# Conditioning projections of a decoder step: from split fp32r products to plain fp32 matmuls in four column strips

## What is computed

```python
sh1, sc1, g1, sh2, sc2, g2 = split(silu(c) @ ada_w[layer] + ada_b[layer], 6)
h = rmsnorm(x, gain) * (1 + sc1) + sh1
x = x + g1 * mixer(h)
...
shift, scale = split(silu(c) @ kv_ada_w + kv_ada_b, 2)         # shared K/V
shf, scf = split(silu(c) @ final_ada_w + final_ada_b, 2)       # last norm
```

## Time and profile before

| | |
|---|---|
| median of 3 runs | 2059.22 us (2056.70 to 2061.25) |
| span of the profiled execution, first to last instruction | 2059.2 us |
| TensorE, VectorE, ScalarE busy | 91%, 75%, 61% of the span |
| GpSimd busy | 5% |
| HBM traffic over the span | 251 GB/s |
| expert loop, 1107 to 2032 us (first expert left out) | 925 us, clock 1.00, DMA 329 GB/s |

### The profile page before, as it was taken

How to read it: one execution, slowest core, us unless ns; L and a number is a source line. 1 busy time by engine, 2 the same in 40 slices (tenths; PEclk the granted TensorE clock), 3 DMA queues, 4 the chain that set the end, 5 groups by cost and what they waited for, 6 DMA issues and landing times.

```text
span 2059.2 us, 26798 instructions
## 1 busy us (share of the span) xinstructions
PE 1882.6 (91%) x9526; PEld 1462.0 (71%) x9526; DVE 1538.1 (75%) x2020; ACT 1251.1 (61%) x1490; POOL 101.5 (5%) x112
## 2 busy tenths in 40 slices
PE   5799996899898976976999999999999999999996
PEld 2696454888798734164787877878778787787784
DVE  5473777676585487263898989989899898898993
ACT  5553444566334434053777777777777777777773
POOL 2000010000000030001000000000000000000000
PEclk9897777999999859985999999999999999999998
DMA  9254693488444350433898998989989999899990
GB/s 312 82 195 157 233 316 131 149 277 270 164 153 155 123 206 1 162 129 119 287 363 319 340 363 303 359 320 341 366 304 355 336 329 364 300 359 335 328 355 21
DMA packets 230616, 518.84 MB, mean 252 GB/s; under 512 B 5187, under 2 KB 27817, under 8 KB 230546
## 3 DMA queue, kind: packets, MB, share of 16 engines
q1 hardware_dynamic: 226386, 504.42, 68.5%
q0 software_dynamic: 3856, 12.40, 1.7%
q10 hardware_dynamic: 304, 1.08, 0.2%
HBM read 509.91 MB, written 7.96 MB: 251 GB/s over the span
## 4 chain that ended last, share of the span: by engine, by line
PE 76%; DVE 10%; ACT 5%; issue 5%; DMA 3%; SPq 1%; DVEq 0%; POOL 0%; ACTq 0%; POOLq 0%
PE psum L609 18%; PE psum L611 18%; PE psum L610 18%; PE psum L581 3%; PE psum L582 3%; DVE w_lo L1374 2%; DMA ring<-in_moe_w_gate_up 2%; PE psum L954 2%; PE psum L852 2%; SPq L376 1%; PE psum L969 1%; PE psum L776 1%; DVE x L1462 1%; PE psum L599 1%; PE psum L705 1%
## 5 line engine op out<-in xcount | busy, mean ns | idle before, releaser
L1788 DVE TENSOR_TENSOR w_lo<-ring,w_hi 128x1024 fp32r<-128x1024 f32 x672 | 815.8, 1224 | 120.5 <-ACT w_hi L1326 109.4
L1326 ACT CAST w_hi<-ring 128x1024 fp32r<-128x1024 f32 x672 | 704.1, 1052 | 230.8 <-PE psum L611 230.8
L1374 DVE TENSOR_TENSOR w_lo<-ring,w_hi 128x1024 fp32r<-128x1024 f32 (+1 forms) x260 | 311.0, 1214 | 181.9 <-ACT w_hi L1068 181.0
L1068 ACT CAST w_hi<-ring 128x1024 fp32r<-128x1024 f32 (+1 forms) x260 | 265.7, 1040 | 249.8 <-PE psum L582 110.6
L609 PE MATMUL psum<-w_hi,xe_hi 128*128 128x512 f32 x896 | 371.1, 414 | 4.3 <-DVE w_lo L1788 4.3
L611 PE MATMUL psum<-w_hi,xe_lo 128*128 128x512 f32 x896 | 354.4, 396 | 0.0
L610 PE MATMUL psum<-w_lo,xe_hi 128*128 128x512 f32 x896 | 354.0, 395 | 0.0
L609 PE MATMUL psum<-hh,w_hi 128*128 128x264 f32 x864 | 252.1, 292 | 22.3 <-DVE hl L1443 13.6
L610 PE MATMUL psum<-hl,w_hi 128*128 128x264 f32 x864 | 248.1, 287 | 0.0
L611 PE MATMUL psum<-hh,w_lo 128*128 128x264 f32 x864 | 247.8, 287 | 0.0
L609 PEld LDWEIGHTS psum<-w_hi,xe_hi 128*128 128x128 f32 x896 | 169.2, 189 | 41.8 <-DVE w_lo L1788 4.7
(11 more groups left out here) (300 smaller groups left out, 2126.3 us busy)
## 6 DMA issues: line engine op xcount, KB each, us to landing
ring<-in_moe_w_gate_up SPq DMA_DIRECT2D x112, 2048.0 KB, 7.9
ring<-in_moe_w_down SPq DMA_DIRECT2D x56, 2048.0 KB, 7.6
ring<-in_ada_w SPq DMA_DIRECT2D x24, 2048.0 KB, 9.4
ring<-in_ffn_w_gate_up SPq DMA_DIRECT2D x22, 1024.0 KB, 7.0
ring<-in_gla_w_in SPq DMA_DIRECT2D x6, 2048.0 KB, 7.9
ring<-in_ffn_w_down SPq DMA_DIRECT2D x5, 2048.0 KB, 8.9
ring<-in_kv_ada_w SPq DMA_DIRECT2D x4, 2048.0 KB, 11.4
ring<-in_kv_w SPq DMA_DIRECT2D x4, 2048.0 KB, 8.1
```

Of the source, the lines that this page charges most:

```text
L1068: eng.copy(unit(w_hi, kind, m, ks), quarter(slot(kind, i), kind, m % 4, ks)).then_inc(S["hi_ready"], 1)
L1326: eng.copy(unit(w_hi, kind, n), quarter(ring[(BASE + j // 4) % RING], kind, j % 4)).then_inc(S["hi_ready"], 1)
L1374: eng.tensor_tensor(unit(w_lo, kind, m, ks), quarter(slot(kind, i), kind, m % 4, ks), unit(w_hi, kind, m, ks), ALU.subtract).then_inc(S["l ...
L1788: eng.tensor_tensor(unit(w_lo, kind, n), quarter(ring[(BASE + j // 4) % RING], kind, j % 4), unit(w_hi, kind, n), ALU.subtract).then_inc(S ...
```

## The change

c is kept once in fp32, padded with zeros to 32 columns (`c_pad`). The array's 128 columns are taken as four strips of 32; strip g multiplies row chunks g and 4 + g of the tile, straight from the ring slot, as plain fp32, and writes PSUM rows 32 g to 32 g + 31 of one bank. The four matmuls of a half tile have different chunks as moving data and stand next to each other in the program. Nothing of a conditioning tile is split any more; the four unit buffers serve the other kinds only, whose numbers close up. Its slot comes free when the four last matmuls are done (`ada_done`). The turn becomes a plain fp32 matmul with the full 128 rows of `ada_row` as weights and `strip_sum` as moving data, a matrix of ones that adds the four strips while it transposes; GpSimd builds it from the identity at the start. VectorE's second add goes away. Where conditioning tiles stood ahead of a kind, its first three units are split by a call of their own (`first_splits`), for gla_in behind tile 3 and ahead of the first norm, for gla_out at the place of tile 19.

```diff
-CR = LO_ROW + NC9
+STRIP = 32
+STRIPS = P // STRIP
...
-SPLIT = [t for t in STREAM if t[0] not in ("k_cache", "v_cache")]
+SPLIT = [t for t in STREAM if t[0] not in ("k_cache", "v_cache", "ada")]
 UNIT_AT = {t: 4 * n for n, t in enumerate(SPLIT)}
-LATE = range(UNIT_AT["sb_out", 0], UNIT_AT["sb_out", 0] + AHEAD)
+LATE = [UNIT_AT[kind, 0] + m for kind in ("gla_in", "gla_out", "sb_out") for m in range(AHEAD)]
...
-        c_split = sb("c_split", [P, KC, CR + 1], F32R)
-        ada_row = sb("ada_row", [CR, 2, 512])
+        c_pad = sb("c_pad", [P, KC, STRIP])
+        strip_sum = sb("strip_sum", [P, NC9])
+        ada_row = sb("ada_row", [P, 2, 512])
...
+            if kind == "ada":
+                return S["ada_done"], STRIPS * (i + 1)
             return S["lo_ready"], UNIT_AT[kind, i] + 4
...
+            eng.wait_ge(S["consts"], 11)
+            for g in range(STRIPS):
+                lo = g * STRIP
+                eng.tensor_copy(strip_sum[lo:lo + STRIP, :], ident[lo:lo + STRIP, lo:lo + NC9]).then_inc(S["consts"], 1)
...
             def ada_turn(i):
                 eng.wait_ge(S["ada_copied"], i + 1)
                 for j in range(4):
-                    last = eng.transpose(pb[ADA_BANKS[i]][:, j * 64:j * 64 + CR], ada_row[:, i % 2, j * P:(j + 1) * P],
-                                         ident[0:CR, 0:CR])
+                    last = eng.matmul(pb[ADA_BANKS[i]][:, j * 64:j * 64 + NC9], ada_row[:, i % 2, j * P:(j + 1) * P],
+                                      strip_sum[:], start=True, stop=True)
                 last.then_inc(S["ada_turned"], 1)
...
-                    has_unit(n)
-                    for k in range(2):
-                        c = c_split[:, 2 * j + k, 0:CR]
-                        to = pb[ADA_BANKS[i]][0:CR, :]
-                        eng.matmul(to, c, unit(w_hi, "ada", n)[:, k, :], start=j + k == 0, stop=False)
-                        last = eng.matmul(to, c, unit(w_lo, "ada", n)[:, k, :], start=False, stop=j + k == 4)
-                    last.then_inc(S["unit_used"], 1)
+                    if j == 1:
+                        landed(eng, "ada", i)
+                    if j % 2 == 1:
+                        for g in range(STRIPS):
+                            k = (j // 2) * STRIPS + g
+                            last = eng.matmul(pb[ADA_BANKS[i]][g * STRIP:(g + 1) * STRIP, :], c_pad[:, k, :],
+                                              cols8(slot("ada", i))[:, k, :], start=j == 1, stop=j == 3)
+                            if j == 3:
+                                last.then_inc(S["ada_done"], 1)
                     if j == 1 and i not in ADA_STARTS:
                         ada_turn(i - 1)
...
-                eng.copy(ada_row[:, i % 2, :], pb[ADA_BANKS[i]][0:CR, :]).then_inc(S["ada_copied"], 1)
+                eng.copy(ada_row[:, i % 2, :], pb[ADA_BANKS[i]]).then_inc(S["ada_copied"], 1)
+            def first_splits(kind):
+                for m in range(AHEAD):
+                    split(UNIT_AT[kind, 0] + m, late=True)
...
-                    split(UNIT_AT["ada", i] + j + AHEAD)
...
             ada(0, 16, ends=True)
+            first_splits("gla_in")
...
-                                  ALU.add).then_inc(S["ada_part"], 1)
-                eng.wait_ge(S["ada_part"], i + 1)
-                eng.tensor_tensor(to, to, got[:, :, LO_ROW:CR], ALU.add).then_inc(S["ada_kept"], 1)
+                                  ALU.add).then_inc(S["ada_kept"], 1)
...
             ada(76, 80, ends=True)
+            first_splits("gla_out")
```

More of the change, by code:

```diff
@@ L22 @@
 NC9 = 1 + NB
-LO_ROW = 32
-CR = LO_ROW + NC9
+STRIP = 32
+STRIPS = P // STRIP
 GH, DK, DV, C = 4, 128, 256, 64
@@ L308, in read_out @@
                 return S["opv_done"], 2 * i + 2
+            if kind == "ada":
+                return S["ada_done"], STRIPS * (i + 1)
             return S["lo_ready"], UNIT_AT[kind, i] + 4
         def quarter(raw, kind, j, ks=4):
-            if kind in ("ada", "up"):
+            if kind == "up":
                 return raw[:].rearrange("p (k c) -> p k c", c=512)[:, 2 * j:2 * j + 2, :]
@@ L323, in unit @@
         def unit(v, kind, n, ks=4):
-            k, c = {"ada": (2, 512), "up": (2, 512), "down": (1, D), "ffn_down": (ks, 256)}.get(kind, (KC, P))
+            k, c = {"up": (2, 512), "down": (1, D), "ffn_down": (ks, 256)}.get(kind, (KC, P))
             return v[n % UNITS][:, 0:k * c].rearrange("p (k c) -> p k c", k=k)
@@ L543, in _ @@
         def _(eng):
-            eng.wait_ge(S["consts"], 11)
+            eng.wait_ge(S["consts"], 11 + STRIPS)
             eng.wait_ge(S["c_silu"], 1)
@@ L1076, in _ @@
             eng.wait_ge(S["c_zero"], 1)
-            eng.copy(c_split[:, :, 0:NC9], pb[5][:, 0:P].rearrange("p (k c) -> p k c", c=16)[:, :, 0:NC9]).then_inc(S["c_hi"], 1)
-            for m in range(AHEAD):
-                split(m)
+            eng.copy(c_pad[:, :, 0:NC9], pb[5][:, 0:P].rearrange("p (k c) -> p k c", c=16)[:, :, 0:NC9]).then_inc(S["c_kept"], 1)
             def ada_copy(i):
-                eng.wait_ge(S["unit_used"], UNIT_AT["ada", i] + 4)
+                eng.wait_ge(S["ada_done"], STRIPS * (i + 1))
                 if i >= 2:
                     eng.wait_ge(S["ada_turned"], i - 1)
-                eng.copy(ada_row[:, i % 2, :], pb[ADA_BANKS[i]][0:CR, :]).then_inc(S["ada_copied"], 1)
+                eng.copy(ada_row[:, i % 2, :], pb[ADA_BANKS[i]]).then_inc(S["ada_copied"], 1)
+            def first_splits(kind):
+                for m in range(AHEAD):
+                    split(UNIT_AT[kind, 0] + m, late=True)
             def ada(lo, hi, ends=False):
@@ L1271, in _ @@
             eng.activation(zs, zs, ACT.Exp).then_inc(S["exps_s"], 1)
-            for m in range(AHEAD):
-                split(UNIT_AT["sb_out", 0] + m, late=True)
+            first_splits("sb_out")
             eng.wait_ge(S["otT_done"], 1)
@@ L1375, in split, with first_splits @@
                                   unit(w_hi, kind, m, ks), ALU.subtract).then_inc(S["lo_ready"], 1)
[L1377 to L1382, removed]
+            def first_splits(kind):
+                for m in range(AHEAD):
+                    split(UNIT_AT[kind, 0] + m, late=True)
+            eng.memset(c_pad[:], 0.0).then_inc(S["c_zero"], 1)
             for k in range(KC):
```

7 lines of the change are left out of this document (3 added, 4 removed).

## The result

The changed kernel takes 2050.68 us (median of 20 runs, 2045.63 to 2060.99), the kernel before in the same session 2060.53 (20 runs): ratio 0.995, with a 95% interval of 0.9939 to 0.9962. That is faster by 9.9 us, where 45.2 were forecast, and 2.7 us above the upper end of the range. The profiled execution has a span of 2050.1 us, against 2059.2 before.

What follows compares the result with a forecast made beforehand. TensorE was taken to bound projections, recurrence, states and feed-forward up, with chains of waits between. Gains 8.2 + 5.1 + 3.9 + 6 + 7.8 + 4.6 + 9.6 = 45.2 us gave 2059.2 - 45.2 = 2014.0, range 1998 to 2048.

Steps and rivals of the forecast that it cites:

- the 7.8 us that were forecast behind the states: Stretch 294 to 344: copy of last output without splits 3.9, square root 2.7, one split fewer 1.2; bounds 3, 10.
- start, table load: Start: path becomes DMA, sqrt table loads at 40.1 instead of 48.27, gain 8.2 us (bounds 5 and 11).
- feed-forward up, first ffn_down load: Feed-forward up: 0.5 us a tile for seven tiles, ffn_down chain 1.1 earlier; gain 4.6 (bounds -8 and 12).
- router, choice of experts: Ahead of the router: norm 5.7 us earlier, expert choice 11.1 instead of 14.5 behind logits; gain 9.6 (bounds 3, 13).
- about 8.4 with the mixed clock: States loop: TensorE time per iteration after the change, 7.5 us at full clock, about 8.4 mixed, against 9.4 today.
- the states term: States loop: shorter iterations and earlier last store, gain taken as 6 us; bounds 0 (DMA already at 87%) and 9.
- the terms of recurrence and tail: Recurrence: a chunk's tile 6.1 to 4.6 us, gain 5.1 (bounds 0, 10); tail: two splits gone, 3.9 (bounds 1, 6).
- rival 3: States loop: clock may fall to 1.2 GHz throughout, 12.1 us an iteration, 22 us lost, total 2042; chance 0.10.
- The strips: Conditioning tiles: four strips overlap fully with a lag, half tile 1.33 us, tile 3.65 against 4.17 at full clock.
- Rivals 1 and 2: Conditioning tiles: strips in series, some 93 us slower, 2152, chance 0.06; starts in order, about 2058, no change, chance 0.10.
- that page's rule on program order: Conditioning tiles: matmuls start and end strictly in program order; by it a tile would be slower than today's.
- rival 4: Early stages: transfers bound them; start gains 5 us, states 0, feed-forward 0, total 2028; chance 0.14.

## Why the prediction was wrong

The sign and most mechanisms were right, the size was not. The table gives the start of the same piece of work in both kernels (us), and what each stage gained. The first 3.9 of the 7.8 us that were forecast behind the states (the copy of the last output) lie ahead of the sum over the heads, so they stand in the row of the states:

| stage, up to | before | after | gain of the stage | forecast |
|---|---|---|---|---|
| start, table load | 48.27 | 40.10 | 8.2 | 8.2 |
| gla_in, first turning of v | 147.26 | 139.38 | -0.3 | 0 |
| recurrence, last update product | 205.91 | 199.46 | -1.4 | 5.1 |
| tail, first broadcast of v | 223.39 | 216.22 | 0.7 | 3.9 |
| states, sum over the heads (L722, L731) | 311.66 | 321.84 | -17.4 | 6 + 3.9 |
| norm and gla_out, next sum of squares | 369.00 | 372.92 | 6.3 | 3.9 |
| feed-forward up, first ffn_down load | 538.16 | 537.35 | 4.7 | 4.6 |
| up to the sum of squares of the last norm before the experts | 904.02 | 902.59 | 0.6 | 0 |
| router, choice of experts | 947.93 | 936.61 | 9.9 | 9.6 |
| the rest of the span | 2059.2 | 2050.1 | -2.2 | 0 |

The gains add up to 9.1. Of the 36.1 us that are missing, 27.3 are in the states and 9.7 in recurrence and tail.

**The step that failed** is "about 8.4 with the mixed clock": the states term took the clock of before for a loop whose TensorE work had changed, and the terms of recurrence and tail (4.6 us a chunk's tile) did the same. What came is rival 3, to which I gave 0.10: 12.75 us an iteration, where it had 12.1, at 1.2 GHz from one end of the loop to the other. Its total, 2042, was still 9 us too low: it counted the gain of recurrence and tail, which did not come either. My argument against it was that no row shows the clock lower where the same tiles are multiplied in less time. The earlier trace rows had the warning in it: the recurrence stood at 0.75 with TensorE busy for 57.94 of 58.65 us, so busy was no protection. Nor was my claim safe that the recurrence cannot lose at half clock: I counted the tile alone, but the unedited products around it slow down as well. The kernels with the multiplies of before show the cause for the states, since they undo the lighter multiplies and leave the turn, the transfers and the missing splits; the part of the recurrence is less sure. Executions whose recurrence code is the same came in two lengths from the first turning of v to the first broadcast: 76.84 us at 0.66 (the changed kernel and the one with six extra matmuls) and 81.6 to 83.3 at 0.62 (five others with strips there; in the three with the one-pass broadcast 1.4 us of it are the wait for the split of v). The rest of the difference, 4.1 to 4.6 us, lies in the first chunk: the changed kernel had the full clock up to 154 us, while the five fell earlier, to between 0.57 and 0.64 in the five microseconds that begin some 5 us behind the first turning of v. What picks between them was not found. The forecast's 9 us of gain are in neither, and the multiplies of before with 78.40 us lie between the two, so that the lighter tile costs time in the recurrence is not shown.

**The strips** were right, and better than I said: what follows a half tile starts 1.00 us behind it (436.68 to 437.68), not 1.33, and the turn takes 0.99 (437.68 to 438.67). Rivals 1 and 2 fall: eight instructions in series take 3.62 us, 3.4 times as long as side by side. The Trainium skill gives 2.38 for three column tiles of the same 32 columns and 512 elements ("TensorE: Matmul & The Clock Gate", Measured speedup vs the span model); the direction agrees. What I drew in the prediction from that page's rule on program order, a tile slower than before, did not come.

**Splits in front of the critical path**: start (table load at 40.10 for a forecast 40.1) and router came within 0.3 us. The norm of the outputs gained 6.3 us where 3.9 were forecast, but the copy of the last output gave less: from the end of the last state product to the sum over the heads it is 7.3 us before and 5.5 after (316.30 to 321.84), 1.8 less where 3.9 were forecast, since the clock is low there too. The choice of experts moved from 14.5 to 10.7 us behind the logits (918.49 + 7.39 = 925.88, then 936.61), for a forecast 11.1.

**Feed-forward** was right in total by luck, through two errors. A tile cost 1.0 us less (14.8 us between turns, 422.87 to 437.68, instead of 15.8), not 0.5, in all but one of the intervals (15.4). But around the last turn TensorE's clock fell there as well:

```profile
516.00:524.00 8.00, 8.00 (x43) 8.00 (x43) 1.79 (x3) 1.72 (x4) 0.00 (x0) 0.59 0.01 3
524.00:532.00 8.00, 8.00 (x68) 8.00 (x67) 4.76 (x7) 3.55 (x5) 0.00 (x0) 1.00 0.01 2
```

43 matmuls instead of 68 in eight microseconds is 2.9 us lost against the full clock, at which the kernel before went through the same stretch. **Transfers** (rival 4) did not bound the states: DMA fell to 237 GB/s there.

## What to carry to other kernels

Price a lighter TensorE stage at both clock levels, the unedited instructions beside it too: here a saving of 1.2 us a tile (4.17 to about 3.0 at 2.4 GHz) turned into a loss of 3.4 us an iteration (9.35 to 12.75), because everything in the loop went from a mean of 0.80 to 0.50. Where a profile already shows TensorE busy at 0.6 to 0.8, the clock is a term of the sum and not a rival at the end. If it does fall, look for work to take out of the same loop rather than for work to put in: extra matmuls lost 5 to 9 us, while two products rewritten gained 21 to 23, and the same strips that save little in one place can save much in another (3.50 to 1.08).

## What was not expected of the hardware

TensorE was busy without a gap from 216 to 307 us at 1.2 GHz; the same loop with about as many instructions ran at 0.50 with four strips side by side, 0.83 with one strip, and 0.82 with sixteen one-pass matmuls over 41 columns behind a recurrence of the same kind, but only 0.70 behind a recurrence with strips, where it took 30 us to rise from 0.50 to 0.84. Plain fp32 matmuls in four column strips of the array overlap almost entirely: four of 512 columns in about the time of one (1.06 us against 3.62 for four in series). And the transfers of the states loop, at 87% DMA share before, still had room: 299 GB/s became 335 where nothing else held them.
